# Turning the decay sums of the state-space heads once and spreading them over the partitions by DMA

## The reference

```
dA = dtc * a                                  # per token and head
cs = cumsum(dA, over the 128 tokens of a chunk)
diff = cs[..., :, None] - cs[..., None, :]
decay = exp(where(causal, diff, -inf))
cb = einsum('bclgn,bcsgn->bcgls', c, b)
y_diag = einsum('bcgls,bcgrls,bcsgrp->bclgrp', cb, decay, xdt)
```

## Time and profile before

| | |
|---|---|
| median of 3 runs | 890.69 us (889.92 to 890.82) |
| the profiled execution | 890.24 us |
| its span, first to last instruction | 888.5 us |
| granted TensorE clock, mean | 0.998 |
| TensorE busy | 870.8 us, 98% |
| DVE busy | 625.2 us, 70% |
| ACT busy | 479.0 us, 54% |
| POOL busy | 156.9 us, 18% |

### The profile page before, as it was taken

How to read it: one execution, slowest core, us unless ns; L and a number is a source line. 1 busy time by engine, 2 the same in 40 slices (tenths; PEclk the granted TensorE clock), 3 DMA queues, 4 the chain that set the end, 5 groups by cost and what they waited for, 6 DMA issues and landing times.

```text
span 888.5 us, 14750 instructions
## 1 busy us (share of the span) xinstructions
PE 870.8 (98%) x6078; PEld 798.3 (90%) x6078; DVE 625.2 (70%) x971; ACT 479.0 (54%) x699; POOL 156.9 (18%) x155
## 2 busy tenths in 40 slices
PE   8999999999999999999999999999999899999997
PEld 8999988898899999999899989888998799999996
DVE  5886996786487655555579999976686575555554
ACT  6864655665475444444664443447675565444443
POOL 1210900000000000000028888660000000000000
PEclk9999999999999999999999999999999999999999
DMA  8654435544455556655566675445543456555551
GB/s 288 188 165 146 140 125 181 170 141 144 161 177 187 192 193 199 195 192 191 177 179 191 184 224 160 151 165 173 178 148 112 145 181 210 197 196 192 190 193 69
DMA packets 82954, 155.27 MB, mean 175 GB/s; under 512 B 6838, under 2 KB 8776, under 8 KB 82888
## 3 DMA queue, kind: packets, MB, share of 16 engines
q1 hardware_dynamic: 82776, 154.29, 53.7%
q10 hardware_dynamic: 112, 0.05, 0.0%
HBM read 152.11 MB, written 1.05 MB: 172 GB/s over the span
## 4 chain that ended last, share of the span: by engine, by line
PE 79%; DVE 14%; DMA 2%; ACT 2%; POOL 1%; issue 1%; DVEq 0%; POOLq 0%; SPq 0%; ACTq 0%
PE ps L561 14%; PE ps L563 13%; PE ps L562 13%; PE ps L629 10%; PE ps L630 10%; PE ps L631 10%; DVE ps L1914 4%; DVE w_lo L1555 3%; DMA raw<-in_ab_w_in 2%; DVE cv L2096 2%; DVE xT L1836 1%; PE ps L687 1%; DVE h_lo L1566 1%; PE ps L937 1%; PE ps L938 1%
## 5 line engine op out<-in xcount | busy, mean ns | idle before, releaser
L1129 ACT ACTIVATE w_hi<-raw 128x1024 fp32r<-128x1024 f32 x284 | 295.7, 1055 | 211.5 <-DMA raw<-in_mlp_w 124.5
L1555 DVE TENSOR_TENSOR w_lo<-raw,w_hi 128x1024 fp32r<-128x1024 f32 x246 | 296.1, 1225 | 114.8 <-ACT w_hi L1129 114.3
L561 PE MATMUL ps<-h_hi,w_hi 128*128 128x256 f32 x1108 | 310.8, 281 | 5.9 <-POOL w_lo L2220 3.8
L563 PE MATMUL ps<-h_hi,w_lo 128*128 128x256 f32 x1108 | 308.4, 278 | 0.0
L562 PE MATMUL ps<-h_lo,w_hi 128*128 128x256 f32 x1108 | 308.4, 278 | 0.0
L561 PEld LDWEIGHTS ps<-h_hi,w_hi 128*128 128x128 f32 x1108 | 209.5, 189 | 8.7 <-POOL w_lo L2220 4.5
L562 PEld LDWEIGHTS ps<-h_lo,w_hi 128*128 128x128 f32 x1108 | 209.4, 189 | 0.1
L563 PEld LDWEIGHTS ps<-h_hi,w_lo 128*128 128x128 f32 x1108 | 208.9, 189 | 0.0
L2249 POOL TENSOR_TENSOR rfac<-stat,mhalf 128x1 f32<-128x1 f32 (+2 forms) x18 | 16.7, 926 | 640.3 <-DVE stat L1810 522.1
L629 PE MATMUL ps<-w_hi,r_hi 128*128 128x512 f32 x256 | 99.8, 390 | 0.0
L630 PE MATMUL ps<-w_lo,r_hi 128*128 128x512 f32 x256 | 99.7, 389 | 0.0
(11 more groups left out here) (282 smaller groups left out, 1250.3 us busy)
## 6 DMA issues: line engine op xcount, KB each, us to landing
raw<-in_mlp_w SPq DMA_DIRECT2D x128, 512.0 KB, 3.7
raw<-in_cd_w_in SPq DMA_DIRECT2D x40, 512.0 KB, 4.0
raw<-in_xa_wkv SPq DMA_DIRECT2D x32, 512.0 KB, 3.7
raw<-in_ab_w_in SPq DMA_DIRECT2D x24, 512.0 KB, 4.7
raw<-in_xa_wq SPq DMA_DIRECT2D x16, 512.0 KB, 3.7
raw<-in_xa_wo SPq DMA_DIRECT2D x16, 512.0 KB, 3.7
raw<-in_cd_w_out SPq DMA_DIRECT2D x16, 512.0 KB, 3.5
raw<-in_ab_w_out SPq DMA_DIRECT2D x12, 512.0 KB, 3.4
```

Of the source, the lines that this page charges most:

```text
L561: nc.tensor.matmul(dst, wt[0], x[0], start=start, stop=False, skip_group_check=True)
L563: return nc.tensor.matmul(dst, wt[1], x[0], start=False, stop=stop, skip_group_check=True)
L1129: nc.scalar.activation(w_hi[:, v % SLOTS, :, :], raw[:, v % SLOTS, :, :], ACT.Copy)\
L1555: V.tensor_tensor(w_lo[:, v % SLOTS, :, :], raw[:, v % SLOTS, :, :], f(w_hi[:, v % SLOTS, :, :]), ALU.subtract).then_inc(lo_ready_dve, 1)
```

## The change

The row pairs leave TensorE. In their place, after the z projection, TensorE turns `cs` once (two transposes, 16 heads on 16 partitions, 256 tokens), ACT copies the result from PSUM to `csT`, SP stores it to a scratch tensor `cs_rows` in device memory, and four DMAs of four heads each (512 KB) copy it from there onto all partitions, into `rowb`. `decay` and the first exponential of `decay_exp` read `rowb` instead of PSUM. The turned sums are those of one chunk each, as the row pairs were. `("csT",)` uses bank 6 ahead of `("cb", 0)`. SP's queue: after raw unit 23 it waits for ACT's copy and issues the store; after raw unit 24 it waits for the store and issues the first broadcast; the others follow raw units 25, 26 and 27. In ACT's queue the copy stands after the last Silu of the conv outputs and ahead of the first Silu of z.

```diff
@@ bank_plan
+    u.append((("csT",), 6))
     u.append((("cb", 0), 6))
     u.append((("cb", 1), 7))
     pair(("pool", 0), (0, 1))
-    for i in range(8):
-        u.append((("rows", i), 6 + i % 2))
-        if i == 0:
-            pair(("K", 0, 0), (2, 3))
-        if i == 4:
-            pair(("K", 0, 1), (0, 1))
+    pair(("K", 0, 0), (2, 3))
+    pair(("K", 0, 1), (0, 1))
@@ SP
+            rows_at = first[("K", 0, 0)]
...
+                if u == rows_at - 1:
+                    sp_.wait_ge(act_made, after("act", "csT"))
+                    sp_.dma_start(cs_rows[:, :], csT[0:HEADS, :]).then_inc(cs_stored, 16)
+                if rows_at <= u < rows_at + 4:
+                    if u == rows_at:
+                        sp_.wait_ge(cs_stored, 16)
+                    h = 4 * (u - rows_at)
+                    sp_.dma_start(rowb[:, h:h + 4, :], cs_rows[h:h + 4, :].unsqueeze(0).broadcast_to([P, 4, T]))\
+                        .then_inc(rows_landed[u - rows_at], 16)
@@ TensorE
             project(("z", 1), [("z", 1, 0), ("z", 1, 1)], h_src)
+            pe.wait_ge(act_made, after("act", "cs"))
+            acquire(("csT",))
+            for t in range(TT):
+                mm = nc.tensor.transpose(bank(("csT",))[0:HEADS, t * P:(t + 1) * P], cs[:, t, :], ident[:, :])
+            mm.then_inc(*finish(("csT",)))
...
-            for i in range(2):
-                project(("pool", 0), pool_banks, h_src, only=[i])
-                row_pair(i)
-            project(("pool", 0), pool_banks, h_src, only=[2, 3])
+            project(("pool", 0), pool_banks, h_src)
...
-                if i + 2 < 8:
-                    row_pair(i + 2)
@@ ACT
             silu_pair(5)
+            act.wait_ge(*full(("csT",)))
+            nc.scalar.activation(csT[0:HEADS, :], bank(("csT",))[0:HEADS, 0:T], ACT.Copy)\
+                .then_inc(act_made, tick("act", "csT"))
+            freed("act", ("csT",))
             for i in range(4):
                 act.wait_ge(dve_made, after("dve", "z", i))
...
-                    nc.scalar.activation(E[:, h % 4, P:2 * P], bank2(("rows", i))[:, h % 2, P:T], ACT.Exp,
+                    nc.scalar.activation(E[:, h % 4, P:2 * P], rowb[:, h, P:T], ACT.Exp,
                                          bias=cs[:, 3, h:h + 1]).then_inc(act_made, tick("act"))
-                freed("act", ("rows", i))
@@ DVE
-                dve.wait_ge(*full(("rows", i)))
+                dve.wait_ge(rows_landed[i // 2], 16)
...
-                    r = bank2(("rows", i))[:, hh, :]
+                    r = rowb[:, h, :]
```

More of the change, by code:

```diff
@@ L292, in trunk @@
             quad_w = sb("quad_w", [64, 32], scope=s)
+        with ExitStack() as s:
+            csT = sb("csT", [T], scope=s)
         k_hi, k_lo = sb("k_hi", [J, T], F32R), sb("k_lo", [J, T], F32R)
@@ L308, in trunk @@
             v_hi, v_lo = sb("v_hi", [TT, D], F32R, s), sb("v_lo", [TT, D], F32R, s)
+        with ExitStack() as s:
+            rowb = sb("rowb", [HEADS, T], scope=s)
         with ExitStack() as s:
@@ L371, in trunk @@
         dw_landed, shift_landed = sem("dw_landed"), sem("shift_landed")
+        rows_landed = [sem(f"rows_landed{i}") for i in range(4)]
+        cs_stored = sem("cs_stored")
+        cs_rows = nc.dram_tensor("cs_rows", [HEADS, T], F32)
         gpost_landed = sem("gpost_landed")
```

## The result

The changed kernel is slower. Beside the kernel before its times were 894.98, 896.47 and 898.21 us against 889.92 to 890.82; the ratio is 1.0066 (95% interval 1.0051 to 1.0081). A fourth execution of it, at a mean granted clock of 0.557, took 1442.73 us and stands in no ratio, as does one of the kernel before in a later comparison, with 3084.69 us. In the last comparison, six executions beside eleven of the kernel before, the ratio was 1.0089 (1.0074 to 1.0105). The profiled execution took 894.98 us, the shortest time of all, with a span of 893.2. So the sign was forecast rightly, while 893.5 and the range up to 896.0 were too low: 1.0066 times 890.49 is 896.4.

What follows compares the result with a forecast made beforehand. TensorE, 98% busy, and the DVE were taken to bound the kernel together at L694. Sg: 130.89 + 5.5 - 0.7 - 2.1 + 0.6 = 134.2, L694 3.3 us later, so 890.24 + 3.3 = 893.5 us; range 890.2 to 896.0.

Steps and rivals of the forecast that it cites:

- the sign: Whole kernel: slower was given 64%, same 26%, faster 10%; slower meant above 892.5 us.
- part 4: DVE's chain to the last Sg: 5.5 us later start, -0.7 waits, -2.1 SBUF decays, +0.6 beside POOL, ending at 134.2.
- Where the limit lies: At column sums L694: TensorE, 98% busy, and the DVE arrive together, so a gain on TensorE alone is lost.
- Part 1: TensorE's work: eight row pairs go, 7.1 us; two transposes come in as four records, 0.45 us; alone -6.7 us.
- Part 2, the hold: ACT's queue before the Silus of z: waiting for and copying csT makes first Silu, rounding and w_lo 5.5 us late.
- Part 3: TensorE's timetable from pool unit 20: the whole saving is spent in waits, reaching L694 at 131.0, as before the change.
- Part 5: DMAs: raw loads stay hidden; first broadcast leaves near 77.5, lands at 82.7, 3 us before decay 0.
- The upper bound (3.5): Sixteen decays of pairs 2 to 5 beside POOL's windows: at most 16 x 0.22 = 3.5 us lost; 0.6 was taken.
- The two bounds given for the whole: Whole kernel with both DVE bounds: 890.8 us with a decay gain of 4.2, 895.6 with none and 0.6 beside POOL.
- the shared decays: DVE decays: no gain from SBUF, 895.0 us, or each blocked in POOL's windows, 896.4 us; 14%.

Runs made afterwards that it cites:

- the early turn: Changed kernel with the turn of cs moved from behind z unit 19 to between z units 17 and 18; 891.36 us, ratio 1.0015 to the kernel before.
- the kernel before without windows: Kernel before with POOL's trailing pooling windows not computed and pdiff set to zero; 890.95 us, ratio 1.0004 to the kernel before.
- The hold alone: Kernel before plus only the turn of cs on TensorE and ACT's copy of it, placed as in the change; 895.45 us, ratio 1.0054.
- without windows: Changed kernel with POOL's trailing pooling windows not computed and pdiff set to zero; 889.41 us, ratio 0.9987 to the kernel before.
- the filled Sg: Changed kernel with ten overwritten matmuls ahead of TensorE's wait for Sg at the column sums; 895.48 us, ratio 1.0059 to the kernel before.
- the fillers: Changed kernel with overwritten matmuls in TensorE's waits: 5, 2 and 9 at pool units, 10 ahead of the column sums; 896.08 us against 897.84 for the changed kernel.
- the mixed kernel: Changed kernel with the turn between z units 17 and 18 and rows of pairs 2 to 5 by matmul into PSUM; 889.30 us, ratio 0.9992 to the kernel before.

## Why the prediction was wrong

Two steps failed: part 4 put 0.6 us on the decays beside POOL, where they lost 2.4, and the sum gave TensorE's waits no price, where the clock behind one of them took 1.6 us and more. By the forecast's own steps:

- *Where the limit lies.* Right. TensorE and the DVE end together at L694; the early turn and the kernel before without windows show it, one from each side. (The list of waits has a second one of 0.2 us for an engine's arithmetic, at L561 for w_lo, that the reading passes over. It changes nothing.)
- *Part 1.* Nearly right. The two transposes are two records and not four: 6078 - 64 + 2 = 6016. They cost 0.2 us and not 0.45, so that 6.9 us came off. TensorE's busy time fell by 5.3 only. By an estimate from the stretches above the rest is the clock: 0.28 x 6 = 1.7 us lost in each of two, against 0.17 x 10 = 1.7 in one of the kernel before (530 to 540 us, 0.83).
- *Part 2, the hold.* Right in mechanism and size. The Silu was put at 74.4 and came at 74.27, w_lo 20 at 76.0 and came at 75.86. In part two small errors cancel: TensorE came to the turn at 73.57, 0.2 later than before, and the turn was 0.2 shorter. The hold alone makes 895.45.
- *Part 3.* The waits were put at 0.5, 1.5, 0.7 and 2.2 us; the trace has 0.55, 1.09, 0.46 and 2.16. The 1.4 at unit 25 did not show: the fall of the clock had brought TensorE there as late as its input. Where the clock stayed up it is there, 1.37 us without windows and 1.44 in the filled Sg:

```profile
...
96.78 0.39 PE L575 MATMUL ps<-mem_hi,w_hi 128*128 128x256 f32 x1 [1.44 <-DVE w_lo L1567]
...
```

  Two waits I had not listed: 1.07 us at the y pair at 113.32 (L846), absent without windows, so from what POOL's windows cost the DVE, and 0.75 for mp_lo at 128.47 (L643). They delay nothing, since TensorE is still ahead of Sg.
- *Part 5.* Right: no decay waited. The first broadcast left at 75.83, earlier than the 77.5 of the forecast. The broadcasts took 6.3 to 7.6 us from issue to landing, against 5.2 for the one I took as the model:

```profile
...
DMA to landing us min/median/max: 6.3/6.5/7.6
```

- *Part 4, the DVE beside POOL.* Here is the first term that was mis-sized. Outside the windows a group of decays saved 0.25 us, as worked out. Inside, from start to start of what follows, the four groups took 1.36, 1.55, 1.25 and 1.36, together 5.5, where from PSUM they took 4.2 and unstretched from SBUF they take 3.1 (0.78 each). So 1.4 us was lost against PSUM, where I had won -1.0 + 0.6 = -0.4, and the sharing cost these decays 2.4, where I had 0.6. Besides, the roundings' differences (w_lo) lost 0.6 and the masked multiplies 0.2 more than before. From w_lo 20 to the end of Sg the DVE took 60.85 us; the forecast had 60.4 - 0.7 - 2.1 + 0.6 = 58.2. The gap of 2.6 us is these terms. The reason that I gave for 0.6, that a decay is short, does not hold: the longest decay lost 766 - 278 = 488 ns, the longest masked multiply 1101 - 551 = 550. The upper bound (3.5) was the better value; the true price with the neighbours was about 0.6 + 2.6 = 3.2. The two bounds given for the whole, 890.8 and 895.6, leave that 3.5 out: one has 0 for the sharing, the other 0.6.
- *A term that the sum lacked: the clock.* The forecast let TensorE wait and took waiting as free. Behind the wait at L694 the clock fell, and since the column sums, the norm's row and Rg are on the path there, 1.6 us were lost in the first trace (4.93 against 3.36) and 3.2 in the two others (6.52 and 6.53). With the fillers 1.8 us of the median come back.

For the profiled execution: Sg slipped by 5.8 (5.4 by the hold, 0.46 since the DVE's chain behind it became longer, not shorter) and the clock added 1.6, so that near 187 us the kernel is 7.4 us late. At the end it is 4.7. The difference lies far behind the change. By the starts of the same w_lo the changed kernel is 7.0 late at 496 us, 5.6 at 518 and 4.6 at 605. The profiled execution of the kernel before has a stretch at 530 to 540 us with a granted clock of 0.83 and this one has none there, but that can explain at most the 1.0 us between the last two. Most traces have one or two of these between 530 and 720 us, and they come and go; perhaps that is part of why the profiled 894.98 lies at the low end of the times. The rest of the 2.7 us is open.

The rival "the shared decays" (14%, 896.4) was nearest to what happened; its mechanism is shown by the run without windows and by the mixed kernel. It puts the end of Sg at 134.2 + 2.9 = 137.1, and it came at 136.71. That its time agrees with 896.4 as well is in part luck, since it has no term for the clock and none for what was won back behind 496 us. The rule of the Trainium skill ("SBUF — State Buffer", section "SBUF: two separate sides") that was set beside the forecast would have given the better number. Its account, that one of the two is locked out for a whole instruction, fits the 766 ns of a decay that otherwise takes 278, but the traces show no lock, only the lengths. Beside the two-port mode the same section counts a DVE instruction with two inputs in SBUF, against a GpSimd one that reads SBUF; that is the case of the masked multiplies and of w_lo, which the forecast put under the two-port mode or left out.

## What to carry to other kernels

A wait put into an engine's queue costs what is queued behind it: the copy of 0.37 us cost 5 us because the rounding of the next weights stood behind it, and moving its producer by half a projection took that back. When an engine is relieved, look for the one that arrives with it; here the relief was worth nothing until the DVE was relieved of the hold and of POOL's windows too, and then 5.0 us beside a kernel with the same windows left out. Data moved from PSUM to SBUF to make a DVE operation faster can make it slower while POOL works: look at what POOL does in that very stretch before counting the gain.

## What was not expected of the hardware

Idle time of TensorE can have a price of its own: behind waits of 2.5 us and more at the column sums the granted clock fell to 1.2 GHz in three traces of three, for 1.6 to 3.2 us of lost time, and useless matmuls of 2.3 us in the wait avoided it in three of three. Near 562 us two waits of 2.62 us had no fall behind them, so the price is a risk and no rule. And a turned block of 16 x 256 floats, stored and read back as 512 KB broadcasts, landed 6.3 to 7.6 us after issue while the weights kept streaming, and no engine waited for a weight load between 60 and 145 us.
